# Decoder layer with PEER experts: the second table's rows gathered as four slots of 32 tokens and summed by 32-column matmuls

## The reference

```python
v1, i1 = lax.top_k(s1, 16); v2, i2 = lax.top_k(s2, 16)      # per token and head, 8 heads
best, pos = lax.top_k(v1 + v2 pairs, 16)                    # 16 experts of 16384
gates = softmax(best)
u = take(u_tab, idx)                                        # rows of 2048 floats
act = gelu(einsum('chkd,cd->chk', u, h))
vv = take(v_tab, idx)
y = einsum('chk,chkd->cd', gates * act, vv)
x = x + g2 * y;  out = rmsnorm(x, final_norm_g)
```

## Time and profile before

| | |
|---|---|
| median of 3 runs | 1825.87 us (1825.27 to 1826.82) |
| span of the profiled execution | 1825.3 us; the page gives no other time for it |
| busy TensorE / VectorE / ScalarE / GpSimd | 81% / 63% / 19% / 34% |
| HBM traffic | 716 MB, mean 393 GB/s |
| mean granted TensorE clock | 0.972 of full speed |

### The profile page before, as it was taken

The page is one execution under the profiler, slowest core; times in us unless marked ns, Lnnn a source line. Parts: engine busy times, 40 slices in busy tenths (PEclk is TensorE's granted clock), DMA queues, the critical chain, the costliest instruction groups (busy, mean ns, idle before and its releaser), DMA issues.

```text
span 1825.3 us, 13714 instructions
## 1 busy us (share of the span) xinstructions
PE 1473.6 (81%) x4834; PEld 831.4 (46%) x4834; DVE 1140.9 (63%) x1562; ACT 348.4 (19%) x697; POOL 617.8 (34%) x625
## 2 busy tenths in 40 slices
PE   2979999899898987777777777768777777777776
PEld 2659987888787632232322323224332322232332
DVE  5868886889789755545555555538455555554445
ACT  3004342854201211011110111102011101010110
POOL 0001111000065863444344343428543443433341
PEclk9989999999999999999999999999999999999999
DMA  9999998669699999999999999999999999999995
GB/s 340 386 389 405 400 352 319 240 241 378 255 407 414 421 421 422 422 422 422 421 422 422 422 421 422 421 413 412 422 421 423 422 422 421 422 422 422 421 422 231
DMA packets 138243, 716.45 MB, mean 393 GB/s; under 512 B 11159, under 2 KB 15437, under 8 KB 63693
## 3 DMA queue, kind: packets, MB, share of 16 engines
q0 software_dynamic: 82976, 604.02, 80.2%
q1 hardware_dynamic: 55212, 111.77, 16.6%
HBM read 713.65 MB, written 2.10 MB: 392 GB/s over the span
## 4 chain that ended last, share of the span: by engine, by line
DMA 59%; PE 21%; DVE 9%; POOL 5%; issue 3%; ACT 2%; SPq 1%; DVEq 0%; POOLq 0%; ACTq 0%
DMA u_rows<-in_peer_u,expert 49%; PE ps L925 5%; PE ps L990 4%; PE ps L768 4%; DMA v_rows<-in_peer_v,expert 4%; DVE u_rows L1753 3%; DVE first_acc L454 3%; POOL v_rows L665 3%; DMA ring<-in_w_peer_q 2%; PE ps L762 2%; POOL u_rows L665 2%; DMA ada_first<-in_w_ada 2%; DMA u_rows<-in_peer_v,expert 1%; PE ps L425 1%; PE ps L304 1%
## 5 line engine op out<-in xcount | busy, mean ns | idle before, releaser
L1021 PE MATMUL ps<-v_rows,diag 128*128 128x512 f32 x1960 | 904.0, 607 | 270.3 <-DMA v_rows<-in_peer_v,expert 256.1
L1753 DVE SCALAR_TENSOR_TENSOR u_rows<-u_rows,h 128x2048 f32<-128x2048 f32 x256 | 586.9, 2293 | 520.2 <-DMA u_rows<-in_peer_u,expert 515.6
L1021 PEld LDWEIGHTS ps<-v_rows,diag 128*128 128x128 f32 x1960 | 358.2, 191 | 814.7 <-issue 586.0
L665 POOL DMA_INDIRECT u_rows<-in_peer_u,expert x256 | 284.2, 1110 | 622.8 <-DVE u_rows L1753 577.5
L665 POOL DMA_INDIRECT v_rows<-in_peer_v,expert x249 | 285.5, 1147 | 97.2 <-issue 78.3
L1350 ACT ACTIVATE diag<-ident,hidden 128x128 f32<-128x128 f32 x250 | 89.3, 395 | 847.1 <-PE ps L1021 534.4
L293 DVE SCALAR_TENSOR_TENSOR ada_acc<-ada_late,cact,ada_acc 128x2048 f32<-128x2048 f32 x57 | 133.9, 2348 | 19.2 <-DMA ada_late<-in_w_ada 18.0
L279 POOL DMA_DIRECT2D ada_late<-in_w_ada x61 | 32.3, 530 | 306.2 <-DVE ada_acc L293 265.0
L990 PE MATMUL ps<-h2T,ring 128*128 128x256 f32 x512 | 118.1, 391 | 6.4 <-DMA ring<-in_w_peer_q 6.4
L990 PEld LDWEIGHTS ps<-h2T,ring 128*128 128x128 f32 x512 | 99.8, 197 | 20.8 <-DMA ring<-in_w_peer_q 6.8
L454 DVE SCALAR_TENSOR_TENSOR first_acc<-ada_first,cact,first_acc 128x1024 f32<-128x1024 f32 x60 | 77.0, 1284 | 15.0 <-DMA ada_first<-in_w_ada 9.4
(11 more groups left out here) (273 smaller groups left out, 1264.6 us busy)
## 6 DMA issues: line engine op xcount, KB each, us to landing
ada_late<-in_w_ada POOLq DMA_DIRECT2D x61, 1024.0 KB, 7.8
ada_first<-in_w_ada SPq DMA_DIRECT2D x64, 512.0 KB, 11.6
ring<-in_w_in SPq DMA_DIRECT2D x10, 2048.0 KB, 26.7
ring<-in_w_o SPq DMA_DIRECT2D x8, 2048.0 KB, 16.1
ring<-in_w_peer_q SPq DMA_DIRECT2D x8, 2048.0 KB, 17.3
opened<-in_w_in SPq DMA_DIRECT2D x8, 1024.0 KB, 12.9
u_rows<-in_peer_u,expert POOLq DMA_INDIRECT x256, 32.2
v_rows<-in_peer_v,expert POOLq DMA_INDIRECT x249, 33.9
```

The lines of the kernel that those rows point to most:

```text
L665: nc.gpsimd.indirect_dma_start(buf[:, :], None, table, bass.IndirectOffsetOnAxis(ap=expert[:, q, k:k + 1], axis=0)).then_inc(done, 16)
L1021: ins = nc.tensor.matmul(ps[:, c, :], diag[i % len(diag)][:, :], buf[:, 512 * c:512 * c + 512], start=(n % HALF_SLOTS == 0), stop=last)
L1753: nc.vector.scalar_tensor_tensor(out=buf[:, :], in0=buf[:, :], scalar=1.0, in1=h2[:, q // H, :], op0=ALU.mult, op1=ALU.mult, accum_out=hid ...
```

## The change

Slots are taken in groups of four. A v gather still brings 128 rows of 8 KB. It now holds, for 32 of the tokens, their rows of four slots: buffer c of a group has in partitions 32 i to 32 i + 31 the rows of tokens 32 c to 32 c + 31 of slot 4 m + i. ScalarE rearranges the indices and the weights of each job for this with 16 small copies each (`spread`, `expert_rows`, `weight_rows`). The stationary matrix of a buffer is 128x32, four weighted 32x32 diagonals above each other, made out of `ident32` (a reduction on VectorE ahead of the first retrieval). Its matmul sums the four slots and writes 32 PSUM partitions. For each bank the four buffers follow one another. There are 16 such matrices, a whole job's, in place of 9 full ones. v slots have 8 buffers, used in two groups of four that are freed as a whole; slot 248 has a buffer of its own, and 249 to 255 use `u_rows` buffers, each after the dot that used it. All slots are summed by TensorE.

```diff
-    v_rows = [at(f"v_rows{b}", A + o * KB, [P, D]) for b, o in enumerate((0, 8, 16, 24, 32, 40, 48, 56, 112))]
+    spare_rows = at("spare_rows", A + 112 * KB, [P, D])
+    v_rows = [at(f"v_rows{b}", A + 8 * b * KB, [P, D]) for b in range(8)]
...
-    diag = [at(f"diag{b}", e_next[0] + 512 * b, [P, P]) for b in range(len(v_rows))]
+    diag = [small(f"diag{b}", [P, QUAD]) for b in range(TOPK)]
...
-    BY_VECTOR = tuple(SLOTS - TOPK + k for k in (1, 3, 5, 8, 10, 13))
...
+    def group_used(eng, g):
+
+        if QUADS * g >= LAST:
+            eng.wait_ge(last_used, g - LAST // QUADS + 1)
+        else:
+            eng.wait_ge(v_used[g % 2], g // 2 + 1)
...
+                q, m, c = n // TOPK, n // QUADS % GROUPS, n % QUADS
+                if m == c == 0:
+                    pool.wait_ge(experts_spread, q + 1)
                 buf, landed, _ = next_slot(n, v_rows, v_landed)
-                if n >= LAST:
-                    pool.wait_ge(dots, SLOTS)
-                elif n >= len(v_rows):
-                    used_up(pool, n - len(v_rows))
-                gather(n, buf, landed, peer_v[0])
+                if n > LAST:
+                    pool.wait_ge(dots, n + 1)
+                elif n < LAST and n >= len(v_rows) and c == 0:
+                    group_used(pool, n // QUADS - 2)
+                gather(expert_rows[:, q, m, c:c + 1], buf, landed, peer_v[0])
...
+            def group_products(g, bufs, first, last):
+
+                for k in range(4):
+                    if g == 0:
+                        copied(pe, f"g2b{k}")
+                    if g == HALF_GROUPS:
+                        pe.wait_ge(y_taken, k + 1)
+                    for c in range(QUADS):
+                        rows = slice(QUAD * c, QUAD * c + QUAD)
+                        ins = nc.tensor.matmul(ps[rows, k, :], diag[(QUADS * g + c) % len(diag)][:, :],
+                                               bufs[c][:, 512 * k:512 * k + 512], start=first, stop=last)
+                    if last and k < 3:
+                        ins.then_inc(summed, 1)
+                mark_used(ins, g)
...
+            def spread(dst, src):
+
+                for c in range(QUADS):
+                    for i in range(QUADS):
+                        ins = nc.scalar.copy(dst[QUAD * i:QUAD * i + QUAD, :, c], src[QUAD * c:QUAD * c + QUAD, i:TOPK:QUADS])
+                return ins
...
+                w = weight_rows[:, q % 2, :, :]
+                spread(w, hidden[:, q % 4, :]).then_inc(weights_spread, 1)
+                act.wait_ge(weights_spread, q + 1)
+                for m in range(GROUPS):
+                    if q:
+                        group_used(act, GROUPS * (q - 1) + m)
+                    for c in range(QUADS):
+                        nc.scalar.activation(diag[QUADS * m + c][:, :], ident32[:, :], ACT.Copy,
+                                             scale=w[:, m, c:c + 1]).then_inc(diagonal, 1)
...
+            dve.wait_ge(const_ready, 1)
+            nc.vector.reduce_sum(ident32[:, :], ident[:, :].rearrange("p (c j) -> p j c", j=QUAD), AX.X).then_inc(ident32_ready, 1)
             for part in range(RETRIEVAL):
                 retrieve(part, 0)
...
-            for n in BY_VECTOR:
...
-            step(nc.vector.tensor_tensor(y[:, :], y[:, :], g2b[:, :], ALU.mult))
-            step(nc.vector.tensor_tensor(x2[:, 1, :], x2[:, 1, :], y[:, :], ALU.add))
```

More of the change, by code:

```diff
@@ L59 @@
 SLOTS = TT * H * TOPK
+QJOBS = TT * H
+QUAD = 32
+QUADS = P // QUAD
+GROUPS = TOPK // QUADS
 KB = 1024
@@ L538, in next_slot, with mark_used @@
         return rows[b], landed[b], 16 * (use + 1)
-    def used_up(eng, n):
-        if n >= LAST:
-            eng.wait_ge(last_used, sum(LAST <= i <= n for i in by_tensor))
-        else:
[L545 to L550, removed]
+    def group_used(eng, g):
+        if QUADS * g >= LAST:
+            eng.wait_ge(last_used, g - LAST // QUADS + 1)
+        else:
+            eng.wait_ge(v_used[g % 2], g // 2 + 1)
+    def mark_used(ins, g):
+        ins.then_inc(last_used if QUADS * g >= LAST else v_used[g % 2], 1)
     with nc.Block() as block:
@@ L679, in gather_u @@
                     pool.wait_ge(dots, n - len(u_rows) + 1)
-                gather(n, buf, landed, peer_u[0])
+                q, k = divmod(n, TOPK)
+                gather(expert[:, q, k:k + 1], buf, landed, peer_u[0])
             def gather_v(n):
@@ L1037, in looped @@
-            def looped(first_round, rounds):
-                with nc.Fori(first_round, first_round + rounds, 1, engines=(mybir.EngineType.PE,)) as r:
-                    for b in range(ROUND):
-                        pe.wait_ge(v_landed[b], r * 16 + 16)
-                        pe.wait_ge(diagonal, r * ROUND + (b + 1))
-                        row_products(ROUND * first_round + b, v_rows[b], b)
-            ROUND = len(v_rows)
+                for g in range(lo, hi):
+                    bufs = []
+                    for n in range(QUADS * g, QUADS * g + QUADS):
+                        buf, landed, count = next_slot(n, v_rows, v_landed)
+                        pe.wait_ge(landed, count)
+                        bufs.append(buf)
+                    pe.wait_ge(diagonal, QUADS * g + QUADS)
+                    group_products(g, bufs, g % HALF_GROUPS == 0, g % HALF_GROUPS == HALF_GROUPS - 1)
@@ new lines, in looped @@
+            def looped(lo, rounds):
+                with nc.Fori(lo // ROUND, lo // ROUND + rounds, 1, engines=(mybir.EngineType.PE,)) as r:
+                    for i in range(ROUND):
+                        g, bufs = lo + i, v_rows[4 * (i % 2):4 * (i % 2) + 4]
+                        for c in range(QUADS):
+                            pe.wait_ge(v_landed[4 * (i % 2) + c], r * 32 + 16 * (i // 2 + 1))
+                        pe.wait_ge(diagonal, r * (QUADS * ROUND) + QUADS * (i + 1))
+                        group_products(g, bufs, False, False)
@@ L1342, in _ @@
                     exponent(q + 2)
+                if q + 1 < QJOBS:
+                    spread_experts(q + 1)
+                if q == 0:
+                    act.wait_ge(ident32_ready, 1)
                 act.wait_ge(weighted, q + 1)
-                for k in range(TOPK):
-                    n = TOPK * q + k
-                    if n not in BY_VECTOR:
-                        i = by_tensor.index(n)
-                        if i >= len(diag):
-                            used_up(act, by_tensor[i - len(diag)])
-                        nc.scalar.activation(diag[i % len(diag)][:, :], ident[:, :], ACT.Copy,
-                                             scale=hidden[:, q % 4, k:k + 1]).then_inc(diagonal, 1)
+                w = weight_rows[:, q % 2, :, :]
[4 more added lines that the diff above has]
+                        group_used(act, GROUPS * (q - 1) + m)
+                    for c in range(QUADS):
+                        nc.scalar.activation(diag[QUADS * m + c][:, :], ident32[:, :], ACT.Copy,
+                                             scale=w[:, m, c:c + 1]).then_inc(diagonal, 1)
             nc.scalar.preload_act_table_set("sqrt_and_others")
```

64 lines of the change are left out of this document (26 added, 38 removed).

## The result

The changed kernel took 1829.87 us, the median of 11 runs (1826.82 to 1831.69), against 1825.87 us for the kernel before (11 runs, 1823.30 to 1827.41). The ratio is 1.0019 with a 95% interval of 1.0011 to 1.0027, which is +3.5 us (2.0 to 4.9). That lies within the range of the forecast, 1.4 us under its value, and at the edge of what a measurement of this kernel can tell from no change. The profiled execution took 1830.54 us, 1827.9 of them its span, against 1825.3 us of the kernel before's profile. Outside the span lie 1.8 to 3.0 us in the changed kernel's runs (mean 2.65) and 1.7 to 3.1 in the kernel before's 102 runs of the later jobs (mean 2.3). So most of the difference is in the span, and some 0.3 us of it may not be.

What follows compares the result with a forecast made beforehand. The prediction took DMA gathers at 422 GB/s as the bound. Start 0.3, middle 2.5, tail 1.6 and end 1.0 summed to +5.4 us on 1825.87, giving 1831.3 us, range 1824 to 1845.

Steps and rivals of the forecast that it cites:

- No gain from TensorE: Gathers: they take 1272 us before and after, so the edit acts only where transfers pause or have ended.
- Steady state at no cost: Between first gather and tail: GpSimd's wait for groups, 11.5 us, is hidden behind 22.4 us of queued gathers.
- ScalarE's copies: Each job's 32 small index and weight copies, 7 us of 80, cost nothing; the last job's are hidden by 3 us.
- Two passes at a time: TensorE's groups: two passes overlap, since starts follow queue order; 6.9 us at full clock, 8.6 with the half-speed start.
- rival B: TensorE runs four strips at once, a group takes 5.2 us; total +1.2, 1827.1 us (1825 to 1829.5); chance 0.28.
- forecast's own signs: In the profile: groups of 8 to 9 us and VectorE's last takes 1.7 us apart; groups of 5 mean rival B.
- Start, +0.3: Before the first gather: the added 128x128 reduction delays the first retrieval by 0.3 us, between 0 and 0.6.
- Middle, +2.5: Behind slot 127: GpSimd resumes 5.2 us later; price between 0 and 5.2 us, about half taken, 2.5.
- Tail stall, +1.6: Gather 244 waits for group 59: 11.5 us needed, 9.94 queued, so 1.6 us without transfers.
- End, +1.0: After the last slot: take and sum end at 1818.8 against 1817.9, +1.0 us, with TensorE's clock staying up.

Runs made afterwards that it cites:

- e2: Changed kernel with a group's matmuls ordered strip by strip in place of bank by bank: 1842.56 us, ratio 1.0100 to the kernel before.
- e7: Changed kernel with small matmuls after groups 58 to 62 to keep TensorE's clock up: 1826.99 us, ratio 1.0003 to the kernel before.
- e4: Changed kernel with VectorE's taking of the first tile's sums moved from slot 145 to 151: 1826.68 us, ratio 1.0005 to the kernel before.
- e5: Changed kernel with the edits of e1 and e4 and the ident32 reduction behind the first retrieval: 1826.91 us, ratio 0.9998 to the kernel before.
- e6: Kernel before with the taking of the first tile's sums moved to slot 151, as in e4: 1826.23 us, ratio 0.9994.
- e10: Changed kernel with the edits of e5 and e7 together: 1826.62 us, ratio 1.0006 to the kernel before.
- e1: Changed kernel with the last 12 v slots in other buffers, 8 slots queued behind slot 239 instead of 4: 1827.65 us, ratio 1.0008.
- e8: Changed kernel timed once more in another job, no edit: 1831.17 us, ratio 1.0022 to the kernel before.
- e12: Changed kernel with a second, idle reduction to a scratch tile behind the first retrieval: 1827.81 us, ratio 1.0011 to the kernel before.
- e9: Changed kernel with only the ident32 reduction moved behind the first retrieval: 1826.66 us, ratio 1.0002 to the kernel before.

## Why the prediction was right where it was, and wrong where it was

**No gain from TensorE: right.** 422 GB/s before and after, and TensorE's 550 us less of busy time bought nothing. Steady state at no cost was right too: GpSimd waits for groups, with enough queued behind, and from the first gather to dot 145 it is 696.6 us here and 696.5 before. ScalarE's copies were hidden as reckoned: for the last job they ended at 1775.7 and diagonals were complete at 1779.2, before group 60 landed at 1782.07.

**Two passes at a time: wrong.** This was the step "the second pass of strip 0 waits for its first, and strip 1 can start only beside that second pass". A waiting pass does not hold up the other strips, as e2 shows, until four wait. A group has the eight steps of rival B, and its 5.2 us lie in the 4.9 to 6.6 measured. By the forecast's own signs this is B: groups of about 5 us in place of 8 to 9, and VectorE's last takes 1.33 us apart in place of 1.7. The Trainium skill ("TensorE: Matmul & The Clock Gate", Part 3) has strips overlapping, and the trace agrees (four starts at 1803.17), but its strict order of starts does not hold here: in e2 strip 1 started at 1813.06 while three earlier passes of strip 0 had yet to start. The Trainium skill ("TensorEngine Tiling (Array Packing)", Theoretical Speedup) gives up to 4x for a dimension of 32 or less, and the traces agree: 3.64 us a group in e7 against 13.7, 3.8x.

**Start, +0.3: measured 0.37** for the reduction, in the trace. The first gather was later by 1.68 us in all. The rest is not the reduction's: the output projection had already ended 1.8 us later.

**Middle, +2.5: measured 0 in the profile (0.5 at most).** The delay behind slot 127 was there (4.18 us; the forecast said 5.2), but it has next to no price. Over 1228 to 1244 the mean rate of all DMA engines lacked some 4 us of transfers, and the slots landed on time nevertheless. In nine traces with the stop, dot 145 to slot 239 takes 570.6 to 571.4 us, in the four without it (e4, e5, e6, e10) 570.5 to 570.8; the means differ by 0.4, and by 0.5 among the versions of the changed kernel. The tenth with the stop is e2, whose groups take twice as long, and there the price is 3.5. The forecast's own reckoning had the new gather flow at 1236.8, just ahead of the last queued landing at 1237.0; that was right, and it meant a price of 0. Adding half of the dip to it was the error.

**Tail stall, +1.6: measured 1.2 in the profile,** 0.3 to 1.3 over the traces that have it. The size is near, in part by luck, for it was worked out with a group of 8.6 us. By the forecast's own reckoning a group of 5.2 us should have had no stall (8.1 against 9.94). It has one. The landing of slot 239 is that of the slowest DMA engine, and others ran dry earlier, when slots 240 to 243 were nominally good for 9.9 us: the completion signals of slot 243 come from 1776.36 to 1781.83, and the rate fell to 164 GB/s at 1776. The slowest engine did not stop, since slot 244 completes at 1784.30, 2.47 us after 243. The 1.2 us come behind it: slots 245 and 246 complete 3.09 us apart each, while the DMA moved only 340 and 352 GB/s (1782 to 1786), busy as it was. Why it was slower just then no run here shows. e1 removed the dip and the stall with a deeper queue; e7, with a quicker group, kept a dip of 2 us and had no stall.

**End, +1.0: measured 0** in the profile (7.6 against 7.7 us from the last signal), and 0.7 more where the clock stayed low longer (8.4 in e1 and e8). VectorE's 1.33 us per bank set it at least in part, as in rival B. The forecast had the clock stay up for the last group, and it did not: TensorE rested 3.40 us, the clock fell 2.7 us into that rest (not 4.8, as at the middle of the kernel before), and the group's first steps were 0.85 us long. e7, which kept the clock up, puts 0.9 us on that.

**The sum.** The forecast was 0.3 + 2.5 + 1.6 + 1.0 = 5.4. The steps it named came to 0.4 + 0 + 1.2 + 0 = 1.6: B's total was 1.2. Some 2 us more were measured, which no step had in it; in the profile 1.8 of them stand at the end of the output projection. The range (1824 to 1845) is so wide that 1825.87 + 1.6 = 1827.5 would lie in it too. That the time came near the value forecast, and over the 1829.5 from which the forecast counts it as slower, is luck. That TensorE's clock was lower in the output projection is shown, in both profiles of this program. Why this program meets it there and its near copies don't is open, and so is whether it does in every run: a second idle reduction (e12) and a moved one (e9) both went with a quick stage, but one profile each does not prove that they caused it.

## What to carry to other kernels

An engine that becomes four times quicker beside a DMA bound shows up as nothing, and its idle time lowers its clock just where it is next on the path. When buffers are freed in groups, look at the last place where the wait has only its own group queued behind it: the stall is there, and it begins before the nominal queue is used up. A dip of the mean DMA rate is not yet a loss: measure it between two landings of numbered transfers. Differences of 0.1% need the span cut into stages in several profiles, because a stage with no changed code can hold them.

## What was unexpected of the hardware

- Matmuls of 32 columns into four strips start together (1803.17) although each has a second pass to come. With eight passes of a strip in a row, the next strip starts with the fifth pass, while three wait.
- A rate of 123 GB/s for 4 us in the middle of the gathers cost 0.5 us or less of landing time, and 164 and 123 GB/s for 2 us each in the tail 1.2 us.
- One of the 16 DMA engines ran 4 to 5 us behind the others (1226.90 against 1231.99, 1234.46 against 1238.68), and it alone sets when a gather of 1 MB has landed.
- In the same stage with TensorE busy throughout, the granted clock over 425 to 430 us was 0.66 in one program and 0.50 in another, and 0.91 in a third that came there earlier (e9): where the slow phases fall moved this stage by 2 to 3 us.
- Gathers waited 20 us in the queues in place of 32 to 34 with no change of rate.
